# Mixture-of-experts outputs added into a transposed residual in SBUF instead of by scatter-add DMAs

## The reference, cut to what matters

```python
def run_block(args):                       # 32 rows of one expert
    xb_i, e = args
    return clamped_swiglu_expert(xb_i, w_gu[e], b_gu[e], w_down[e], b_down[e])
gu = xb @ w_gu + b_gu                      # 1024 -> 2 x 1024
gate = min(gu[:, :D_FF], 7); up = clip(gu[:, D_FF:], -7, 7)
act = (up + 1) * (gate * sigmoid(gate * 1.702))
yb = act @ w_down + b_down                 # 1024 -> 1024
y = zeros.at[row_token].add(yb * row_gate[:, None])
h = h + y
```

## Time and profile before

| | |
|---|---|
| median of 3 runs | 1315.88 us |
| the three runs | 1315.38, 1315.88, 1318.69 us |
| span of the profiled execution | 1315.0 us |
| TensorE matmul busy | 1194.6 us (91%) |
| VectorE, ScalarE, GpSimd busy | 525.5, 338.0, 258.9 us |
| moved by DMA | 446.42 MB |
| granted TensorE clock, mean | 0.964 |

### The profile page before, as it was taken

The page is one execution under the profiler, slowest core; times in us unless marked ns, Lnnn a source line. Parts: engine busy times, 40 slices in busy tenths (PEclk is TensorE's granted clock), DMA queues, the critical chain, the costliest instruction groups (busy, mean ns, idle before and its releaser), DMA issues.

```text
span 1315.0 us, 31271 instructions
## 1 busy us (share of the span) xinstructions
PE 1194.6 (91%) x12045; PEld 553.5 (42%) x12046; DVE 525.5 (40%) x1335; ACT 338.0 (26%) x693; POOL 258.9 (20%) x372
## 2 busy tenths in 40 slices
PE   7999999999999979797997999999987787999794
PEld 5874555856444323232342334444432232333231
DVE  1337856556433323242342444333432232433231
ACT  3136565322122212121221222222221111222121
POOL 1000003000222222222221222223221121222121
PEclk9999999998999989998997999999999898999898
DMA  5132144179899999999999999999999999999992
GB/s 183 46 120 64 33 103 136 56 318 395 324 417 418 420 420 421 419 421 420 421 419 419 417 413 418 418 420 420 419 420 423 423 421 423 419 366 423 423 420 99
DMA packets 59873, 446.42 MB, mean 339 GB/s; under 512 B 15360, under 2 KB 27848, under 8 KB 35264
## 3 DMA queue, kind: packets, MB, share of 16 engines
q1 hardware_dynamic: 48736, 424.97, 77.7%
q0 software_dynamic: 8352, 18.77, 5.4%
q10 hardware_dynamic: 2752, 2.23, 0.5%
HBM read 435.24 MB, written 15.07 MB: 342 GB/s over the span
## 4 chain that ended last, share of the span: by engine, by line
PE 64%; DMA 30%; DVE 3%; ACT 1%; issue 1%; ACTq 0%; POOLq 0%; SPq 0%; DVEq 0%
PE PS L1105 30%; DMA W<-in_expert_w_gate_up 29%; PE PS L696 16%; PE PS L1120 14%; PE PSC L696 2%; DMA W<-in_norm_mix_w 0%; PE PS L872 0%; PE PS L706 0%; DVE W L1168 0%; DMA out<-Y,IDXS 0%; DVE W L1341 0%; DVE W L1340 0%; ACT W L457 0%; ACT Y L684 0%; PE PS L1018 0%
## 5 line engine op out<-in xcount | busy, mean ns | idle before, releaser
L1105 PE MATMUL PS<-W,XT 128*32 128x512 f32 x5184 | 606.7, 616 | 92.5 <-DMA W<-in_expert_w_gate_up 86.6
L1105 PEld LDWEIGHTS PS<-W,XT 128*32 128x32 f32 x5184 | 166.6, 112 | 478.3 <-issue 340.6
L1120 PE MATMUL PS<-W,AT 128*32 128x256 f32 x5184 | 299.3, 383 | 2.5 <-DVE SIG L1555 1.7
L684 ACT ACTIVATE Y<-SIG,ident 32x256 f32<-32x256 f32 x324 | 163.8, 506 | 354.1 <-DMA out<-Y,IDXS 290.8
L696 PE MATMUL PS<-W 128*128 128x512 f32 (+6 forms) x874 | 246.4, 440 | 2.1 <-ACT W L621 1.1
L1120 PEld LDWEIGHTS PS<-W,AT 128*32 128x32 f32 x5184 | 171.8, 112 | 155.3 <-issue 57.5
L1530 DVE TENSOR_TENSOR GU<-PS,BGU 128x512 f32<-128x512 f32 x81 | 56.0, 692 | 341.4 <-PE PS L1105 336.0
L696 PEld LDWEIGHTS PS<-W 128*128 128x128 f32 (+1 forms) x874 | 147.3, 193 | 81.9 <-issue 71.4
L436 POOL DMA_INDIRECT out<-Y,IDXS x81 | 112.2, 1385 | 252.8 <-ACT Y L684 249.9
L676 ACT ACTIVATE SIG<-GU 128x256 f32<-128x256 f32 x81 | 33.8, 418 | 414.8 <-DVE GU L1532 414.8
L420 POOL DMA_INDIRECT XG<-hn_scratch,IDXC x81 | 85.3, 1053 | 73.8 <-POOL IDXC L417 68.4
(11 more groups left out here) (294 smaller groups left out, 557.9 us busy)
## 6 DMA issues: line engine op xcount, KB each, us to landing
W<-in_expert_w_gate_up SPq DMA_DIRECT2D x128, 2048.0 KB
W<-in_expert_w_down SPq DMA_DIRECT2D x64, 2048.0 KB
W<-in_w_in SPq DMA_DIRECT2D x10, 1024.0 KB, 5.3
W<-in_x SPq DMA_DIRECT2D x8, 512.0 KB, 11.2
W<-in_w_out SPq DMA_DIRECT2D x2, 1024.0 KB, 9.8
W<-in_w_out SPq DMA_DIRECT2D x1, 2048.0 KB, 7.7
hn_scratch<-W POOLq DMA_DIRECT2D x4, 512.0 KB, 13.3
out<-W ACTq DMA_DIRECT2D x4, 512.0 KB, 12.8
```

The lines of the kernel that those rows point to most:

```text
L684: ins = a.activation(Y[0:BT, QW * j:QW * j + QW], SIG[js, :], ACT.Copy, scale=GATEB[js, bass.ds(at, 1)])
L1105: last = pe.matmul(GPS[32 * j:32 * j + 32, :].rearrange("p (g n) -> p g n", g=2), XT[:, 32 * k:32 * k + 32], rhs, start=(k == 0), stop=(k ...
L1120: last = pe.matmul(DPS[32 * j:32 * j + 32, :], AT[:, 32 * k:32 * k + 32], DNW[p][:, k, j * QW:(j + 1) * QW], start=(k == 0), stop=(k == KD ...
```

## The change

The residual is kept transposed in SBUF for the whole second part: `ACC`, 128 partitions by 8 x (512 + 32), holds feature 128k+p of token n at partition p, column (k, n); 32 columns behind the tokens take padding rows. The copies that made `HNT` now write there. The stores of `H[t]` to `out` are gone, and so are `y_scale`, `scatter` and the index tables for it. A table `TOK` (block by row, integers) says which token each row belongs to. For each block VectorE folds the gate into the activation (L1536 becomes an operation with a column of `GATEB`) and into the bias, writes the down product to PSUM, and transposes it in 32 x 32 squares into `YT`. The down weights are read with another column order so that this is the wanted transpose. Then VectorE adds rows 0 to 15 and GpSimd rows 16 to 31, one instruction of 128 x 8 elements for each row, at a column whose number was loaded into a register. `GU` now lies in PSUM. Behind the last block TensorE transposes `ACC` back, ScalarE and VectorE copy it out, and SyncE stores four tiles.

```diff
@@ names and memory
-        GU = sb("GU", 2 * QW)
-        Y = sb("Y", D)
+        YT = sb("YT", QW)
+        ACC = sb("ACC", KD * COLS)
+        ACCV = ACC[:, :].rearrange("p (k n) -> p k n", k=KD)
+        TOK = sb("TOK", BT, I32)
+        GU, YG = PSC[:, :, 0:QW], PS[7][:, 0:QW]
+        GATED, UP = GU[:, 0, :], GU[:, 1, :]
+        def tokens_of(engine, i, m0):
+            at = within(i, MAXB, "no routing gives more than MAXB blocks")
+            row = TOK[0:1, m0:m0 + HALF]
+            row = TOK[at:at + 1, m0:m0 + HALF] if isinstance(i, int) else bass.at_runtime_partition(row, at)
+            return nc.values_load_multi_w_load_instructions(row, engines=[engine], min_val=0, max_val=COLS - 1,
+                                                            skip_runtime_bounds_check_because="a token, or a column behind the last one")[1]
@@ SyncE
-                sp.dma_start(BDN[p][0:P:32, :], b_dn[e].rearrange("(j n) -> j n", j=4)).then_inc(S_(f"bdn_in{p}"), 16)
+                sp.dma_start(BDN[p][0:P:32, :].rearrange("j (c x) -> j c x", c=KD),
+                             b_dn[e].rearrange("(c j x) -> j c x", c=KD, j=4)).then_inc(S_(f"bdn_in{p}"), 16)
-            sp.wait_ge(S_("h_out"), 16 * NT)
+            sp.wait_ge(S_("tok_ready"), NT + 1)
-            nb = sp.value_load(LASTB[0:1, NE - 1:NE], min_val=NE - 1, max_val=MAXB - 1) + 1
-            sp.wait_ge(S_("scattered"), nb * 16)
-            sp.sem_inc(S_("passed"), 1)
+            for t in range(NT):
+                sp.wait_ge(S_("op_a"), t + 1)
+                sp.wait_ge(S_("op_v"), t + 1)
+                sp.dma_start(out[t * P:(t + 1) * P, :], OP[t]).then_inc(S_("out_done"), 16)
+            sp.wait_ge(S_("out_done"), 16 * NT)
@@ GpSimd
-            def scatter(i):
...
-                g.indirect_dma_start(out=out, out_offset=bass.IndirectOffsetOnAxis(ap=IDXS[0:BT, :], axis=0),
-                                     in_=Y[0:BT, :], in_offset=None, compute_op=ALU.add,
-                                     bounds_check=S - 1, oob_is_err=False).then_inc(S_("scattered"), 16)
+            def add_tokens(i):
+                toks = tokens_of(g.engine, i, HALF)
+                g.wait_ge(S_("yt_ready"), i + 1)
+                if not (isinstance(i, int) and i == 0):
+                    g.wait_ge(S_("v_added"), i)
+                    g.wait_ge(S_("g_added"), i)
+                for m in range(HALF):
+                    col = ACCV[:, :, bass.ds(toks[m], 1)]
+                    ins = g.tensor_tensor(col, col, YTV[:, :, HALF + m:HALF + m + 1], ALU.add)
+                ins.then_inc(S_("g_added"), 1)
             with g.Fori(1, ahead + 1) as i:
                 next_gather(i + 3)
-                scatter(i)
+                add_tokens(i)
@@ ScalarE
-                    a.activation(HNT[:, 4 * half:4 * half + 4, :], h4(PS[2 + half]), ACT.Copy).then_inc(S_("ht_ready"), 1)
-                a.dma_start(out[t * P:(t + 1) * P, :], H[t]).then_inc(S_("h_out"), 16)
+                    a.activation(ACCV[:, 4 * half:4 * half + 4, t * P:(t + 1) * P], h4(PS[2 + half]), ACT.Copy).then_inc(S_("ht_ready"), 1)
-            def y_scale(i):
...
-            with a.Fori(2, nb) as i:
+            with a.Fori(1, nb) as i:
                 sigmoid(i)
-                y_scale(i - 1)
-            y_scale(last)
+            for t in range(NT):
+                a.wait_ge(S_("op_ps"), 2 * t + 1)
+                a.activation(OP[t][:, 0:512], OPS[2 * t % 4], ACT.Copy).then_inc(S_("op_a"), 1)
@@ TensorE
-                        last = pe.matmul(DPS[32 * j:32 * j + 32, :],
-                                         AT[:, 32 * k:32 * k + 32],
-                                         DNW[p][:, k, j * QW:(j + 1) * QW],
+                        rhs = DNW[p][:, k, :].rearrange("p (c q x) -> p q c x", c=KD, q=4)[:, j]
+                        last = pe.matmul(DPS[32 * j:32 * j + 32, :].rearrange("p (c x) -> p c x", c=KD),
+                                         AT[:, 32 * k:32 * k + 32], rhs,
+            pe.wait_ge(S_("v_added"), last + 1)
+            pe.wait_ge(S_("g_added"), last + 1)
+            for n in range(2 * NT):
+                t, half = n // 2, n % 2
+                if t >= 2:
+                    pe.wait_ge(S_("op_v" if half else "op_a"), t - 1)
+                for c in range(4):
+                    ins = pe.transpose(OPS[n % 4][:, c * P:(c + 1) * P], ACCV[:, 4 * half + c, t * P:(t + 1) * P], ident[:, :])
+                ins.then_inc(S_("op_ps"), 1)
@@ VectorE
-            ts(IDXT[0:BT, :], IDX[0:BT, :], 2, None, ALU.logical_shift_right).then_inc(S_("rows_done"), 1)
+            link(ts(TOKF, TOKL, 0.25, float(S), ALU.mult, ALU.add))
+            link(stt(out=TOKP, in0=TOKL, scalar=0.0, in1=IO32[0:MAXB + 1, :], op0=ALU.is_equal, op1=ALU.mult))
+            tt(TOK[0:MAXB + 1, :], TOKF, TOKP, ALU.add).then_inc(S_("tok_ready"), 1)
-                tt(SIG[:, :], SIG[:, :], GU[:, 0:QW], ALU.mult).then_inc(S_("glu"), 1)
+                stt(out=SIG[:, :], in0=SIG[:, :], scalar=gate_of(i), in1=GATED, op0=ALU.mult, op1=ALU.mult).then_inc(S_("glu"), 1)
@@ y_evac
                 v.wait_ge(S_("bdn_spread"), i + 1)
+                toks = tokens_of(v.engine, i, 0)
                 v.wait_ge(S_("d_ps"), i + 2)
-                tt(SIG[:, :], DPS, BDN[p][:, :], ALU.add).then_inc(S_("y_ready"), 1)
+                stt(out=YG, in0=BDN[p][:, :], scalar=gate_of(i), in1=DPS, op0=ALU.mult, op1=ALU.add).then_inc(S_("y_ready"), 1)
+                v.wait_ge(S_("y_ready"), i + 2)
+                if not (isinstance(i, int) and i == 0):
+                    v.wait_ge(S_("g_added"), i)
+                    v.wait_ge(S_("v_added"), i)
+                v.transpose(YT[:, :], YG).then_inc(S_("yt_ready"), 1)
+                v.wait_ge(S_("yt_ready"), i + 1)
+                for m in range(HALF):
+                    col = ACCV[:, :, bass.ds(toks[m], 1)]
+                    ins = tt(col, col, YTV[:, :, m:m + 1], ALU.add)
+                ins.then_inc(S_("v_added"), 1)
@@ behind the last y_evac
+            for t in range(NT):
+                v.wait_ge(S_("op_ps"), 2 * t + 2)
+                v.tensor_copy(OP[t][:, 512:D], OPS[2 * t % 4 + 1]).then_inc(S_("op_v"), 1)
```

More of the change, by code:

```diff
@@ L196, in hybrid_block @@
         GPS, DPS, RPS = PS[0], PS[1][:, 0:QW], PS[6][:, 0:P]
+        GU, YG = PSC[:, :, 0:QW], PS[7][:, 0:QW]
+        GATED, UP = GU[:, 0, :], GU[:, 1, :]
+        ACTV = GATED.rearrange("p (f c) -> p c f", c=NC)
+        YTV = YT[:, :].rearrange("p (k m) -> p k m", k=KD)
+        TOKL = PS[4][0:MAXB + 1, 0:BT]
+        OP = [W0[:, D * t:D * t + D] for t in range(NT)]
+        OPS = [PS[i] for i in (2, 3, 4, 5)]
         def bc(v, n):
@@ L441, in _ @@
             next_gather(2)
-            g.wait_ge(S_("h_out"), 16 * NT)
             next_gather(3)
-            g.wait_ge(S_("rows_done"), 1)
-            scatter(0)
+            g.wait_ge(S_("tok_ready"), NT + 1)
+            g.wait_ge(S_("p_a"), 5)
+            add_tokens(0)
             with g.Fori(1, ahead + 1) as i:
                 next_gather(i + 3)
-                scatter(i)
-            scatter(ahead + 1)
-            scatter(ahead + 2)
+                add_tokens(i)
+            with g.Fori(ahead + 1, ahead + 3) as i:
+                add_tokens(i)
         @block.scalar
@@ L673, in sigmoid @@
                     a.wait_ge(S_("act_ready"), i)
-                if not isinstance(i, int):
-                    a.wait_ge(S_("ys_ready"), i - 1)
-                a.activation(SIG[:, :], GU[:, 0:QW], ACT.Sigmoid, scale=ALPHA).then_inc(S_("sig_ready"), 1)
-            def y_scale(i):
-                at = within(i, MAXB, "no routing gives more than MAXB blocks")
-                a.wait_ge(S_("y_ready"), i + 2)
-                if not (isinstance(i, int) and i == 0):
-                    a.wait_ge(S_("scattered"), i * 16)
-                for j in range(4):
-                    js = slice(BT * j, BT * j + BT)
-                    ins = a.activation(Y[0:BT, QW * j:QW * j + QW], SIG[js, :], ACT.Copy, scale=GATEB[js, bass.ds(at, 1)])
-                ins.then_inc(S_("ys_ready"), 1)
+                a.activation(SIG[:, :], GATED, ACT.Sigmoid, scale=ALPHA).then_inc(S_("sig_ready"), 1)
             sigmoid(0)
-            sigmoid(1)
-            y_scale(0)
-            with a.Fori(2, nb) as i:
+            with a.Fori(1, nb) as i:
                 sigmoid(i)
-                y_scale(i - 1)
-            y_scale(last)
+            for t in range(NT):
+                a.wait_ge(S_("op_ps"), 2 * t + 1)
+                a.activation(OP[t][:, 0:512], OPS[2 * t % 4], ACT.Copy).then_inc(S_("op_a"), 1)
         @block.tensor
@@ L1354, in _ @@
             for b in B:
[L1355 removed]
+                v.transpose(b["U"], b["T"]).then_inc(S_("u_upd"), 1)
             for m in range(len(LEVELS) * NT):
@@ L1521, in _, with gate_of @@
                    ALU.mult).then_inc(S_("tg_ready"), 1)
+            link(ts(TOKF, TOKL, 0.25, float(S), ALU.mult, ALU.add))
```

(6 more changed lines are left out.)

76 lines of the change are left out of this document (31 added, 45 removed).

## The result

The changed kernel takes 1284.36 us (median of 4 runs, 1283.17 to 1285.02) where the kernel before takes 1315.64 in the same comparison: 0.9754 of it, 95% interval 0.9742 to 0.9766. The prediction was 1286.0. The profiled execution has a span of 1281.4 us and a time of 1283.17; in all four executions 1.7 to 1.8 us lie around the span.

What follows compares the result with a forecast made beforehand. The DMA queues were taken to bound the expert stage, TensorE only locally. Span 1315.0 - 38 (stage) + 0.5 (start) + 7 (end) = 1284.5, median 1286 us; own range 1270 to 1300, wider range 1268 to 1345.

Steps and rivals of the forecast that it cites:

- signs of being wrong: Expert stage: VectorE or GpSimd chained for whole blocks, TENSOR_LOAD near 5 us, q8 packets after 450 us, slow down products.
- What the scatters cost: DMA queues in the expert stage: removing the scatter-adds frees 40 us of engine time, bounds 20 and 42 us.
- The rival in which bytes alone count: DMA queues: the scatters cost only their bytes, 20 us gained in place of 38; 1304 us, chance 0.08.
- What of it becomes time: Expert stage: of 40 us freed, 2 us lost where TensorE never waits; 38 us gained, bounds 20 and 42.
- The start: Before the expert stage: residual stores moved, three small token-table operations added; +0.5 us, or -5 if the stores counted.
- 5.5 + L + 16a: VectorE per block: 5.5 us, L for loading 16 registers (2.0), 16 additions at a (0.11 each); 9.3 us.
- The cover: Expert stage: TensorE's 10.4 us a block hides VectorE; from the DMA engines' 11.4, each 0.1 us costs 8 us.
- The slow rival: VectorE becomes the bound: register load paid per register, 5.0 us, 12.3 us a block; 1361 us, chance 0.20.
- Code loading: VectorE's longer two-expert loop refetches code in 15 rounds, up to 4.8 us each; 1296 us, chance 0.07.
- The down product: TensorE: down weights read in runs of 32, not 256, make it half as slow again; 1339 us, chance 0.04.
- GpSimd: Per block: 16 additions at 0.22 us, 3.5 us, plus the register load; 7.7 us in all, hidden.
- The end: After the last down product: last additions, closing transposes, copies and stores replace GpSimd's drain; +7 us, bounds 0 to 19.

## Why the prediction was right, step by step

**The bound.** Right. The stage was read as a limit of the DMA queues, with TensorE the limit locally. Without the scatters the same 928 us come out whether the outputs are added on chip or not at all. One of the prediction's signs of being wrong did appear, VectorE in the chain for whole blocks, four times ahead of loads. As a sign it was badly chosen: the prediction itself had said that loads would be issued behind `y_free` and the DMA engines stay fed, and so it was.

**What the scatters cost.** The prediction took 40 us of the DMA engines' time. By the pages, q0's share falls from 5.4% of 1315.0 us (71.0 us) to 2.1% of 1280.6 (26.9) when the scatter is gone, 44 us (to about 1, by the rounding of the shares), and to 3.8% of 1297.4 (49.3) when it writes without adding, 22 us. The upper bound, 0.33 us for each of 2048 rows, 42 us, was the better value. The rival in which bytes alone count is dead: the plain write moves the same bytes and gains 17.8 us in the stage.

**What of it becomes time.** The term was -38 and measured -35.8 us to the last down product, -37.8 to the last gate/up product, which leaves the new end out. The mechanism held and two sizes were off against each other, which is luck: 44 us of engine time in place of 40, and about 0.82 of it turned into time (36.2 of 44.1 without the scatter, 17.8 of 21.7 with the plain write) in place of 0.95. The prediction took 2 us off for the stretch in which TensorE is the bound; 8 were lost. The queues show the form of the loss: q1's share rose from 94.1 to 98.3%, by 4.5%, but its bytes by 3.5%. Each byte of weights took the engines about 0.9% longer than before, and that is 8 of 928 us. It goes with what q0 holds. With q0 at 6.5, 4.5, 2.3 and 2.3% (before, plain write, no scatter, changed), share times 790 us over q1's MB is 2.347, 2.359, 2.365 and 2.369. The less q0 holds, the longer each byte of weights takes. One reading is that while an adding packet holds its engine the packets of the others pass faster, so that taking it away does not give all of its time back. That is not shown.

Pauses that look like loads standing at the buffers, the prediction's reason for its 2 us, are in the traces too, and small. In pieces of 10 us the share falls to 0.97 and 0.98 in two places of the changed kernel, some 0.5 us in all. The kernel before loses 3 us so, not between 720 and 940 us but in its other long stretch without a load in the chain, which the prediction's mean of 1.00 over 950 us had hidden. First two rows of the kernel before, then two of the changed one:

```profile
1150.00:1160.00 10.00, 10.00 (x132) 4.13 (x128) 3.76 (x11) 2.44 (x5) 2.93 (x4) 1.00 0.80 319
1160.00:1170.00 10.00, 9.82 (x128) 3.80 (x120) 3.48 (x9) 2.44 (x5) 2.75 (x4) 1.00 0.90 357
```

```profile
860.00:870.00 10.00, 10.00 (x128) 4.18 (x124) 6.22 (x28) 0.38 (x1) 4.08 (x18) 1.00 0.97 395
920.00:930.00 10.00, 10.00 (x132) 4.29 (x128) 6.24 (x27) 0.38 (x1) 4.09 (x18) 1.00 0.98 384
```

**The start.** +0.5 predicted, -0.9 measured (-0.4 and -0.1 in the two other executions); the bound of -5 for the residual's stores was not touched, and taking them out alone was worth nothing.

**VectorE.** 5.5 + L + 16a was put at 9.3 us, measured 8.2. L was 1.13 in place of 2.0. The additions took 1.96 in place of 1.8, 0.122 each. The two transposes from PSUM took 0.45 each where the earlier trace rows had 0.65 from SBUF. Together -0.87 + 0.16 - 0.4 = -1.1. The Trainium skill, Runtime: NRT & Kernel Launch, section Instruction fetch mechanics, gives about 200 ns a register for loads from HBM, also in bulk. For this load from SBUF the measurement decides: 1.13 us for 16, 0.31 for one, so some 0.055 for each further register.

**The cover.** Here a step failed without hurting the sum. "At L + 16a = 4.9 the cover is used up; at 5.9 VectorE reaches the 11.4 of the DMA engines" promised that a block of 10.4 us is free and one up to 11.4 nearly so. Four more transposes made it 10.4 us and cost 15, 12.7 of them in the stage. The step compared means. Its 4.2 us a block held the biases' shuffles only as a mean, and not the sequencer's work between experts, and TensorE now has 257 us in which no load helps to cover, so that whatever VectorE takes beyond 10.4 us is lost there. As an estimate, the cover is about 1.5 us a block: 10.3 us of TensorE, less 8.2 and the 0.65 (11.05 - 10.4) that the changes of expert add on average.

**The slow rival.** Its condition, the load paid by the register, did not hold. Single loads, the nearest that was built, are far dearer than its 1361: 1652. L is then 6.9 and not 5.0, since each load has its address operation and a gap, and 14 rounds fetch code at nearly 7 us each. What one instruction with L = 5.0 would cost is not shown.

**Code loading.** Not in the changed kernel: from 410 to 1250 us q1 and q0 alone carry anything. But the rival was a real neighbour, and its price of "up to 4.8" us a round was too low. The Trainium skill, Runtime: NRT & Kernel Launch, section Instruction fetch mechanics, states that a branch to instructions that are no longer held must fetch them first. The kernel with eight more transposes agrees: it waits at the loop's return, 7.27 us in full queues, and nowhere else in the round that long.

**The down product.** L1118 takes 382 ns on average with its columns read in runs of 32, L1120 took 383: nothing.

**GpSimd.** 0.177 us an addition (2.83 / 16) against 0.22; hidden.

**The end.** Here too a step failed without hurting the sum. The prediction left the last down product where it was. In fact that product waits 3.17 us for VectorE's bias addition, which stands behind the register load, and then takes 5.21 us at a granted clock of 0.69. From the end of the last gate/up product to its own end there are 11.8 us in place of 9.8: +2.0, which the parts above count to the stage. Behind it 14.9 us follow where 18.4 had been laid out. Up to the end of VectorE's last transpose they are 2.5 less (L is 1.13, and work came to lie beside the slow product), GpSimd's additions 0.5 and the closing transposes 0.6 less. From the last gate/up product to the end of the span the change costs 26.8 - 21.6 = 5.1 us (by unrounded times), where +7 was forecast.

**The sum.** Span 1284.5 predicted; 1281.4 in the profiled execution and 1282.4 to 1283.3 in the three others. The median came out at 1284.36 against 1286. That it is so near is in part luck: more engine time and less of it turned into time, a cheaper load and a dearer last product.

## What to carry to other kernels

Where the DMA queues are the bound, price each kind of packet by the engine time that it takes in the trace and not by its bytes: a row added in HBM took twice a row written. Work moved to an engine with slack is free only up to the slack in the tightest stretch, with everything counted that comes once for each expert or round. And a longer loop can come to fetch its code in every round: four more transposes at each `y_evac` left VectorE's loop free of it, eight more cost 7 us a round. Look for the instruction queues in the stage when a loop has been made longer.

## What the runs showed of the hardware that was not expected

- A fetch of code behind full DMA queues stopped VectorE for about 7 us (7.27 at 499.9 us of the kernel with eight more transposes), at 13 of 14 returns to the loop's top.
- In the changed kernel a transpose of 128x256 in 32 x 32 squares took 0.45 us with its input in PSUM (L1556, L1574) and 0.65 with it in SBUF (L1536). A clamp of the same size went the other way: 0.43 us in PSUM (L1543), 0.29 in SBUF (L1532 of the kernel before).
- A plain 4 KB row held a DMA engine for 0.16 us and left the stage's rate at 425 GB/s; an added one held it for 0.33 us, and the rate was 418.
- In the profiled execution of the kernel without the scatter, the mixer lost about 9 us ahead of the stage, and TensorE ran at a granted clock of 0.55 between 226 and 256 us, near the lower of its two levels, 1.2 of 2.4 GHz, busy 29.48 us of 30. First that row, then the same stretch of the changed kernel:

```profile
226.00:256.00 30.00, 29.48 (x283) 25.71 (x284) 14.12 (x33) 6.86 (x16) 0.00 (x0) 0.55 0.25 89
```

```profile
226.00:256.00 30.00, 29.11 (x372) 26.22 (x372) 17.49 (x38) 10.71 (x23) 0.00 (x0) 1.00 0.26 90
```

  The same program had executions of 1270 to 1273 us besides this one of 1282.4, and the kernel before has single ones near 1325 among many near 1317. What brings the clock down there was not tried.
